# A two-block transformer kernel on one core: the MLP and the expert stage put in one program block, pooling means as band products on TensorE, tile 0's queries with tokens as the stationary operand

## The reference, cut to what matters

```python
m = square(relu(rms_norm(x, pre_mlp_g) @ mlp_w1)) @ mlp_w2      # first block's MLP
x = x + rms_norm(m, post_mlp_g)
h = concatenate([meta_tokens, x])                               # 16 + 256 rows

def pool_mixer(h, w_pool, scale):      # windows 2, 4, 8, 16, one for each 256 channels
    pooled = (c - c_prev) / minimum(pos + 1, w) - hg            # trailing mean minus self
    outs.append(einsum('bsc,cd->bsd', pooled, w_pool[g]))
    return concatenate(outs) * scale
h = h + pool_mixer(rmsnorm(h, norm_mix[0]), pool_w[0], pool_scale[0])

def peer(h, w_query, sub_keys, u, v):  # 8 heads, 2 x 128 sub-keys, 16 experts of 16384
    q = (h @ w_query) as (token, head, half, 128)
    s = einsum('bthpc,hpnc->bthpn', q, sub_keys)                # then top-16 of each half,
    ...                                                         # top-16 of their 256 sums
    return einsum('btk,btkd->btd', gate * gelu(u[expert] . h), v[expert])
h = h + peer(rmsnorm(h, norm_ffn[0]), peer_wq[0], peer_keys[0], peer_u[0], peer_v[0])
```

## Time and profile before

| | |
|---|---|
| median of 3 runs | 1946.3 us (1945.75 to 1946.77) |
| the profiled execution, its time | 1945.45 us |
| its span, first to last instruction | 1943.7 us |
| PE, DVE, ACT, POOL busy | 72%, 59%, 31%, 27% of the span |
| moved by DMA | 669.98 MB, mean 345 GB/s |
| chain that ended last | DMA 35%, PE 19%, DVE 13% |

### The profile page before, as it was taken

One profiled execution on the slowest core, in us unless ns is written; L12 is line 12 of the kernel. 1 busy time (PEld: TensorE's weight loads), 2 busy tenths in 40 slices (PEclk: granted clock), 3 DMA queues, 4 the chain that ended last, 5 costly groups with the idle time before them and its releaser, 6 DMA issues.

```text
span 1943.7 us, 20478 instructions
## 1 busy us (share of the span) xinstructions
PE 1406.8 (72%) x6422; PEld 591.3 (30%) x6422; DVE 1154.7 (59%) x2667; ACT 604.8 (31%) x1567; POOL 519.5 (27%) x572
## 2 busy tenths in 40 slices
PE   6978999968666655658967786578678865556565
PEld 5835666557223210112312232122132221101010
DVE  2551000073787766676678655776786568777764
ACT  2041111122334322334344332333444233232332
POOL 2000000001434333333233332323333233333332
PEclk9988999968888876669977897789778886776666
DMA  9022345314999999999999999999999999999997
GB/s 336 34 112 98 139 163 205 140 54 177 420 421 421 421 419 420 420 419 403 417 420 387 400 418 419 421 390 417 420 396 406 418 422 417 421 421 421 421 422 292
DMA packets 113366, 669.98 MB, mean 345 GB/s; under 512 B 11359, under 2 KB 12513, under 8 KB 44401
## 3 DMA queue, kind: packets, MB, share of 16 engines
q0 software_dynamic: 76032, 553.68, 69.0%
q1 hardware_dynamic: 37232, 115.09, 15.6%
HBM read 667.68 MB, written 1.05 MB: 344 GB/s over the span
## 4 chain that ended last, share of the span: by engine, by line
DMA 35%; PE 19%; DVE 13%; ACT 4%; issue 3%; DVEq 2%; POOL 2%; ACTq 1%; POOLq 0%
DMA big<-in_peer_uv,expert 32%; PE ps L558 7%; DVE big L571 6%; PE ps L719 6%; DMA normed<-in_peer_uv,expert 3%; DVEq L457 2%; PE ps L345 2%; POOL big L524 2%; PE ps L543 1%; ACT placed L603 1%; DMA big<-in_w_kv 1%; ACT placed L607 1%; ACT L579 1%; PE ps L723 1%; ACT L603 1%
## 5 line engine op out<-in xcount | busy, mean ns | idle before, releaser
L558 PE MATMUL ps<-big,placed 128*32 128x512 f32 (+1 forms) x2056 | 625.3, 809 | 417.2 <-ACT placed L607 415.1
L571 DVE CUSTOM_DVE_ANT_0 big<-big,ps 128x1024 f32<-128x1024 f32 x514 | 613.9, 1219 | 333.7 <-DMA big<-in_peer_uv,expert 317.2
L524 POOL DMA_INDIRECT big<-in_peer_uv,expert x514 | 489.7, 953 | 980.5 <-PE ps L558 874.0
L603 ACT ACTIVATE placed<-sel,dots 128x32 f32<-128x32 f32 (+1 forms) x528 | 168.3, 319 | 815.5 <-DVE dots L571 808.3
L558 PEld LDWEIGHTS ps<-big,placed 128*32 128x32 f32 (+1 forms) x2056 | 83.6, 122 | 861.0 <-ACT placed L607 780.2
L719 PE MATMUL ps<-big 128*128 128x512 f32 x384 | 189.3, 630 | 11.0 <-DVE big L1041 4.7
L607 ACT ACTIVATE placed<-placed,gate 128x32 f32<-128x32 f32 (+1 forms) x528 | 169.5, 321 | 37.1 <-issue 1.0
L230 DVE RECIPROCAL stats<-stats 128x1 f32<-128x1 f32 (+1 forms) x17 | 2.7, 162 | 253.3 <-ACT stats L224 252.8
L1538 PE MATMUL ps<-ua,big 128*128 128x256 f32 x512 | 116.7, 383 | 0.0
L1549 PE MATMUL ps<-big,sc 128*128 128x512 f32 x256 | 114.4, 592 | 0.0
L719 PEld LDWEIGHTS ps<-big 128*128 128x128 f32 x384 | 70.2, 197 | 126.3 <-issue 108.3
(11 more groups left out here) (296 smaller groups left out, 1242.2 us busy)
## 6 DMA issues: line engine op xcount, KB each, us to landing
big<-in_mlp_w SPq DMA_DIRECT2D x16, 2048.0 KB, 7.8
big<-in_w_kv SPq DMA_DIRECT2D x32, 512.0 KB, 15.5
big<-in_peer_wq SPq DMA_DIRECT2D x32, 512.0 KB, 13.5
big<-in_w_in SPq DMA_DIRECT2D x5, 2048.0 KB, 17.7
big<-in_peer_uv,expert POOLq DMA_INDIRECT x514, 15.3
big<-in_peer_wq SPq DMA_DIRECT2D x1, 8192.0 KB, 27.3
big<-in_w_q SPq DMA_DIRECT2D x16, 512.0 KB, 10.8
big<-in_w_o SPq DMA_DIRECT2D x16, 512.0 KB, 11.8
```

The source lines that it names most:

```text
L524: nc.gpsimd.indirect_dma_start(out=pair_row(n), out_offset=None, in_=rows, in_offset=bass.IndirectOffsetOnAxis(ap=expert[:, n // TOPK % DE ...
L558: last = nc.tensor.matmul(acc[r:r + tokens, :], placed[:, n % RING, 0:tokens], pair_row(n)[:, D + BANK * half:D + BANK * (half + 1)], star ...
L571: nc.vector.tensor_tensor_reduce(out=row, in0=row, in1=rows_x, scale=1.0, scalar=0.0, op0=ALU.mult, op1=ALU.add, accum_out=dots[:, u % 2, ...
L603: a.activation(to, same, ACT.Gelu, scale=dots[:, u % 2, k:k + 1])
```

## The change

- The MLP block and the expert block become one: no barrier, and work of the second can stand ahead of, or among, the end of the first. POOL builds four band matrices (and their parts for the 16 rows before a tile) while the MLP runs; the meta rows are normed then too, ACT's part of it ahead of its release of the `up` banks to PE. SP's loads of `pool_w`, the scale, the `ffn0` gain and the keys move ahead, each behind a wait for its buffer.
- Pooling: transposes, copies, doublings and ratio go. PE takes the normed rows as the stationary operand against the band matrix (128 columns) and, for the 16 rows before the tile, a second small one (16 columns), `pool_sums`; the result is the pooled and transposed tile, and DVE only multiplies by the gain (`pooled_out`).
- Queries of x0: the 128 tokens are the stationary operand and 512 columns of `peer_wq` move (`query_rows_pe`), 2 banks for each half of the heads; ACT brings them out, PE transposes them back by 128 x 128 (`query_columns_pe`), ACT and DVE bring those out. Unit 0's scores stand after the first half.
- The meta queries leave the head. They are products of 16 columns, four in each of the quarters 2 to 5; the meta scores stand in quarter 6, and x1's queries move from quarters 4 to 19 to quarters 6 to 21. x1's norm stands on DVE after unit 0's `route`, its transposes are PE's last work of the head, its copies stand in quarter 1.
- POOL waits ahead of slots 4, 6 and 7 for what these buffers held.

```diff
-        def act_squares(act, tiles, after, tag):
...
+        def act_squares(act, rows, t, tag, scratch):
+            step(act, nc.scalar.activation(scratch[0:rows], h[0:rows, t, :], ACT.Square,
+                                           accum_out=stats[0:rows, t:t + 1]), tag + "_squares")
+            act_root_mean(act, rows, t, tag)
...
+        def ffn0_transposes_out(dve, n):
...
+            dve.wait_ge(S("ffn0_t"), n + 1)
+            if t == NT:
+                nc.vector.tensor_copy(hnt[:, :, 0:META], cut(bank(b), 0, KD, META)).then_inc(S("ffn0_t_out"), 1)
+                return
+            for j in range(2):
+                nc.vector.tensor_copy(hnt[:, 4 * j:4 * j + 4, at:at + P], cut(bank(b + j), 0, 4, P))\
+                    .then_inc(S("ffn0_t_out"), 1)
...
+        def query_rows_pe(pe, half):
+            if half:
+                pe.wait_ge(S("ffn0_scores_out"), 1)
+            for b in range(2):
+                at = D * half + BANK * b
+                for k in range(KD):
+                    last = nc.tensor.matmul(bank(6 + b), hnt[:, k, META:META + P], wq_peer[:, k, at:at + BANK],
+                                            start=(k == 0), stop=(k == KD - 1))
+                last.then_inc(S("q_rows_done"), 1)
+        def query_rows_act(act, half):
+            for b in range(2):
+                act.wait_ge(S("q_rows_done"), 2 * half + b + 1)
+                nc.scalar.activation(query_rows[half][:, BANK * b:BANK * (b + 1)], bank(6 + b), ACT.Copy)\
...
+        def query_columns_pe(pe, half):
+            if half:
+                pe.wait_ge(S("q0_out"), 2)
+            for b in range(2):
+                pe.wait_ge(S("q_rows"), 2 * half + b + 1)
+                for c in range(4):
+                    hp = 4 * b + c
+                    last = nc.tensor.transpose(bank(4 + b)[:, P * c:P * (c + 1)],
+                                               query_rows[half][:, P * hp:P * (hp + 1)], ident[:])
+                last.then_inc(S("q0_t"), 1)
...
+        def late_query(t, hp):
+            return (hp, 0, META) if t == NT else (2 * PH + hp, META + P, P)
...
+            n, at, cols = late_query(t, hp)
             if n >= 2:
                 pe.wait_ge(S("ffn0_q_out"), n - 1)
             for k in range(KD):
-                last = nc.tensor.matmul(bank(4 + hp % 2)[:, 0:cols], wq_peer[:, k, P * hp:P * (hp + 1)],
+                last = nc.tensor.matmul(bank(4 + n % 2)[:, 0:cols], wq_peer[:, k, P * hp:P * (hp + 1)],
                                         hnt[:, k, at:at + cols], start=(k == 0), stop=(k == KD - 1))
             last.then_inc(S("ffn0_q_done"), 1)
...
+            n, at, cols = late_query(t, hp)
+            act.wait_ge(S("ffn0_q_done"), n + 1)
+            head = hp // 2
+            to = q_meta[:, hp % 2, head, META * head:META * (head + 1)] if t == NT else qt[:, hp, at:at + cols]
+            nc.scalar.activation(to, bank(4 + n % 2)[:, 0:cols], ACT.Copy).then_inc(S("ffn0_q_out"), 1)
...
+            if n < META_UNIT:
+                pe.wait_ge(S("q0_out"), 2 * half + 2)
+            else:
+                pe.wait_ge(S("ffn0_q_out"), q_ready)
...
-            pe_transposes(pe, LAYER0_TILES, "ffn0")
+            ffn0_transposes(pe, 0)
+            pe.wait_ge(S("ffn0_t_out"), 2)
+            pe.wait_ge(S("peer_wq0_loaded"), 16)
+            query_rows_pe(pe, 0)
+            ffn0_transposes(pe, 1)
+            query_columns_pe(pe, 0)
+            pe.wait_ge(S("keys0_loaded"), 16)
+            scores0_pe(pe, 0)
+            query_rows_pe(pe, 1)
+            query_columns_pe(pe, 1)
+            scores0_pe(pe, 1)
...
             unit_rows(pe, 0)
-            for n in range(2, 9):
-                scores0_pe(pe, n, 2 * PH)
+            for n in range(2, META_UNIT):
+                scores0_pe(pe, n)
+            ffn0_transposes(pe, 2)
...
+            for n in range(2):
+                act.wait_ge(S("h1"), n + 1)
+                act_squares(act, *FFN0_TILES[n][0:2], "ffn0", ua[:, 0:D])
+            query_rows_act(act, 0)
+            query_columns_act(act, 0, 0)
+            scores0_act(act, 0)
+            act.wait_ge(S("h1"), 3)
+            act_squares(act, *FFN0_TILES[2][0:2], "ffn0", sc[:, 1024:2048])
+            query_rows_act(act, 1)
+            for b in range(2):
+                query_columns_act(act, 1, b)
+            for n in range(1, META_UNIT):
                 scores0_act(act, n)
...
-        LATE_QUERIES = 4
+        LATE_META, LATE_QUERIES = 2, 6
...
+            if LATE_META <= x < LATE_META + 4:
+                if x == LATE_META:
+                    pe.wait_ge(S("ffn0_t_out"), 5)
+                    pe.wait_ge(S("q_meta_zeroed"), 1)
+                for i in range(4):
+                    queries0_pe(pe, NT, 4 * (x - LATE_META) + i)
             hp = x - LATE_QUERIES
+            if hp == 0:
+                scores0_pe(pe, META_UNIT, 2 * PH)
...
+                if n == 4:
+                    pool.wait_ge(S("q0_t"), 4)
                 if n == 6:
-                    pool.wait_ge(S("ffn0_scores_done"), META_UNIT + 1)
+                    pool.wait_ge(S("ffn0_normed"), 3)
+                if n == RING - 1:
+                    pool.wait_ge(S("ffn0_t"), 3)
...
+            ffn0_norm(dve, 2)
...
+                    if (s, j) == (0, 1):
+                        ffn0_transposes_out(dve, 2)
...
+                sp.wait_ge(S("up_done"), DFF // P - FT)
+                sp.dma_start(poolw, pool_w[0].rearrange("g (k p) n -> p (g k) n", p=P)).then_inc(S("pool_w_loaded"), 16)
+                sp.wait_ge(S("down_done"), DFF // P)
+                sp.dma_start(scale_row, pool_scale[0].partition_broadcast(P)).then_inc(S("scale_loaded"), 16)
+                sp.wait_ge(S("down_done"), DFF // P + FT)
+                sp.dma_start(ffn0_row, norm_ffn[0].partition_broadcast(P)).then_inc(S("ffn0_gain_loaded"), 16)
+                sp.wait_ge(S("x2"), NT)
+                sp.dma_start(gb[:, :, :].rearrange("p a n -> p (a n)"), peer_keys[0]).then_inc(S("keys0_loaded"), 16)
+                sp.wait_ge(S("ffn0_scores_done"), L0_UNITS)
...
+                for i in range(POOL_GROUPS):
+                    w = 2 ** (i + 1)
+                    for to, cols in ((band, P), (before, META), (meta_before, META), (meta_band, META)):
+                        band_step(g.memset(to[:, i, :], 1.0 / w))
+                    for to, cols, base in ((band, P, 0), (meta_band, META, 0)):
+                        band_step(g.affine_select(out=to[:, i, :], in_=to[:, i, :], compare_op=ALU.is_ge, fill=0.0, base=0,
+                                                  pattern=[[1, cols]], channel_multiplier=-1))
+                    for to, cols, apart in ((band, P, 0), (before, META, P), (meta_before, META, META), (meta_band, META, 0)):
+                        band_step(g.affine_select(out=to[:, i, :], in_=to[:, i, :], compare_op=ALU.is_ge, fill=0.0,
+                                                  base=w - 1 - apart, pattern=[[-1, cols]], channel_multiplier=1))
+                    band_step(g.affine_select(out=band[:, i, :], in_=band[:, i, :], compare_op=ALU.not_equal,
+                                              fill=1.0 / w - 1.0, base=0, pattern=[[-1, P]], channel_multiplier=1))
...
+                act.wait_ge(S("meta_loaded"), 16)
+                act_squares(act, META, NT, "pool", sc[:, 3072:3072 + D])
...
+                pool_norm(0, META, NT, hnm)
+                dve.wait_ge(S("gain1_loaded"), 16)
+                scaled(0)
+                added(0)
+                scaled(1)
+                pool_norm(1, P, 0, hn[:, 0, :])
+                added(1)
+                pooled_out(0, 1)
+                pool_norm(2, P, 1, hn[:, 1, :])
+                pooled_out(0, 2)
+                dve.wait_ge(S("scale_loaded"), 16)
+                add_mixed(0)
+                pooled_out(1, 3)
+                pooled_out(2, 4)
+                pooled_out(2, 5)
+                dve.wait_ge(S("ffn0_gain_loaded"), 16)
+                ffn0_norm(dve, 0)
+                ffn0_transposes_out(dve, 0)
+                add_mixed(1)
+                add_mixed(2)
+                ffn0_norm(dve, 1)
+                ffn0_transposes_out(dve, 1)
+                query_columns_dve(dve, 0, 1)
+                peer_vector(dve)
...
+                def pool_sums(n):
...
+                    for k in range(KD):
+                        cols = slice(P * k, P * (k + 1))
+                        if t == NT:
+                            last = m.matmul(bank(4)[:, META * k:META * (k + 1)], hnm[:, cols], meta_band[:, k // 2, :],
+                                            start=True, stop=True)
+                            continue
+                        to = bank(6 + k // 4)[:, P * (k % 4):P * (k % 4 + 1)]
+                        m.matmul(to, hn[:, t, cols], band[:, k // 2, :], start=True, stop=False)
+                        last = m.matmul(to[:, 0:META], earlier[:, cols], apart[:, k // 2, :], start=False, stop=True)
```

(14 more changed lines are left out.)

328 lines of the change are left out of this document (134 added, 194 removed).

## The result

The changed kernel takes **1960.9 us** (median of 4 runs, 1958.5 to 1961.6) against 1946.0 for the kernel before on the same chip (4 runs, 1945.4 to 1946.8): a ratio of 1.0074, 95% interval 1.0056 to 1.0091. It is slower by 15 us where 13 us less were forecast. The profiled execution took 1961.45 us, its span is 1959.7; that of before is 1943.7.

A forecast was written before the change was run, and what follows sets the result against it. It took the DMA fetch stream as the bound: its start and whether it runs dry. Gains 14.1 + 2.6 less 3 make 13.7, booked as 13.0, so median 1933.3 us; forecast range 1929.5 to 1938.

The forecast's parts named there:

- The rule it read first: Whole kernel: faster arithmetic in the loop buys nothing; what counts is when the fetch stream begins and whether it runs dry.
- The failed term: Loop quarters 2 to 5: meta queries moved there cost the stream 3 us, with ends of 0 and 24.
- At full clock the following quarters keep pace: Quarters after the first with meta queries: 9.5 us of PE each against the stream's 10.0; at half clock each loses 6.
- The price of an instruction: Meta queries in quarters 2 to 5: a 16-column instruction costs 0.08 us at full clock, 0.13 at half.
- the slot values: Quarters 2 to 5 on PE: four cost 4.2 us at full clock, 7.7 at half.
- rival (d): Quarters 2 to 5: clock stays at 0.50, 16 us a quarter, 24 us lost against 16.7 gained, 1953 us; chance 0.05.
- the start of the band products: Head, pooling: PE can start its first band product at about 392.3 us.
- the chain behind them: Head, after the first query rows: bank copy, transposes, copy, scores, copy, from 432.2 to 435.1 us for `route`.
- x0's sums: Head, pooling: x0's band products take 6.0 us at half clock, within 4.0 to 8.0.
- I take full clock from about 399: Head, pooling: PE working without a break from 392.3 reaches full clock then; x0's pool products take 3.5 us.
- The charge of 1.8 us: Head, query rows: added to each half for a lower clock after the break at the copies, 3.6 in all.
- The unit rows: End of the head, PE: rows of unit 0 take 1.9 us, as before, ahead of six units' scores.

The follow-up runs named there:

- the filled kernel: Changed kernel with the operands of x0's second band product filled with zero rows from 16 to 128 partitions, meta queries left in quarters 2 to 5: 1960.5 us, 1.0095.
- the 144-column experiment: Changed kernel with each meta query product of quarters 2 to 5 moving 144 columns instead of 16, only 16 kept: 1942.6 us, ratio 0.9980.
- riding, wide sums: Changed kernel with meta queries moved along with x1's, x0's second band operands zero-filled to 128 partitions, and that product moving 128 columns: 1927.6 us, ratio 0.9928.
- five kernels with unfilled sums and the new query rows: Changed kernel 1960.9 us; its variants without meta queries 1937.6, with 144-column meta queries 1942.6, meta queries behind slot values 1971.2, meta queries moved with x1's 1940.4.
- the old queries (unfilled and filled): Changed kernel's pooling with tile 0's queries as before the change: 1958.3 us; the same with x0's second band operands zero-filled to 128 partitions: 1949.3 us.
- the four filled kernels with the new query rows: Zero-filled x0 operands on the changed kernel 1960.5 us; with meta queries moved with x1's 1930.8; on that, 128 moving columns 1927.6, or x0's transposes first 1932.5.
- the kernel whose loop kept pace: Changed kernel with meta queries moved along with x1's and x0's second band operands zero-filled to 128 partitions: 1930.8 us, 0.9945, against 0.9968 without the filling.

## Why the prediction was wrong, step by step

**The rule it read first** holds: when the stream begins, and whether it runs dry. The table above puts a number on it, and every span follows it.

**The failed term: the meta queries, "3 us lost, with ends of 0 and 24".** Measured 22.5. The step that failed is the clock: "At full clock the following quarters keep pace" supposed that a busier PE gets it. The trace has PE busy 40.00 of 40 us at 0.59, and at 0.50 in the filled kernel. Where the clock was full in this place (144 columns), a quarter took 10.6 us and the stream lost 3.4.

The price of an instruction, 0.08 and 0.13 us, was wrong too. It was read from transposes of 16 partitions and 16 columns, the nearest row by its columns and the wrong one: band products show 0.214 at half and 0.113 at full clock, with 16 columns or with 128, when both operands have 128 partitions. That is 1.6 and 1.4 times the price taken. But the slot values were priced too high, by a row of a single one: four in a run take 2.6 us at full clock and 3.6 at half, not 4.2 and 7.7. The two errors nearly cancel, and that was luck: a quarter is 7.2 + 2.6 = 9.8 us at full clock (an estimate from these rows; no run has 16 columns at full clock there) where 9.5 was forecast, and 17.3 at half, measured in the filled kernel, where 16.0 was. The Trainium skill, "TensorE: Matmul & The Clock Gate", Part 2, LDWEIGHTS, which prices a weight load by the stationary operand's columns whatever moves, was set aside for that row. At full clock these rows side with it: 0.113 us measured against an estimate of 0.107 from its formula for 128 columns, and no change from 16 to 128 moving columns. At half clock they show twice its figure.

**That was rival (d)**: PE at half clock for most of quarters 2 to 5, 14.0 to 17.3 us a quarter for its 16, decision once more than 17 us are lost. It had a chance of 0.05, argued down with queries in a row that gave 1.00 after 4 us. But those had 144 columns; the 144-column experiment gets its 1.00 in this very place, the 16-column ones do not. Its time, 1953, was 8 us short because the head gained less than it assumed: 24 lost against 16.7 gained there, 22.5 against some 6 here.

**The head.** Right: the start of the band products (7.1 us behind the MLP for 7.0), the query rows (14.0 for 14.1), the chain behind them. Wrong: x0's sums 10.05 for 6.0, outside the stated 4.0 to 8.0, because the price was sought between zero and the 128-column one, and alternating with a 16-partition operand costs more than either; and "I take full clock from about 399", worth 2.7 in x0's pool products, 3.1 in x1's sums and 2.3 in the last ones. The charge of 1.8 us for each half of the query rows was not needed. Together the query rows begin 12.4 us late, and the pooling saves nothing up to there. The first fetch comes 3.6 us earlier than before, counted from the MLP's end, and not 14.1. The kernel with both repaired (riding, wide sums) has its query rows 31.9 us behind the MLP (31.0 forecast), its first fetch 60.3 (61.3), its first dot product 73.9 (76.5), and a ratio of 0.9928 where the forecast was 0.9935. So the working of the chain was sound, and two prices and the clock were not.

**The unit rows** took 3 us longer than before in the changed kernel, with "issue" ahead of four groups of L606 between 462 and 465; the forecast had them at 1.9. They take 5.2 to 5.4 us in all five kernels with unfilled sums and the new query rows, 9.0 and 9.5 with the old queries (unfilled and filled), and 1.93 in the four filled kernels with the new query rows. So the filling alone does not remove it. What does was not tried.

Not settled: the cause of these waits, and what keeps the clock up in pooling in one execution of the unfilled sums and not in others.

## What to carry to other kernels

Price a small matmul by both operands: what it moves may cost nothing, and what it loads may be all of it; a row for a price must have the same partitions on both sides, not the same column count. Before work of narrow products is moved into a loop that has slack "on PE", work its time out at half clock, and let it ride as extra columns on a product that is there anyway. And test an earlier start against the first refill of the ring: here the same filling, a first fetch 8 us earlier, was worth some 4.5 us in the kernel whose loop kept pace and nothing in the one whose loop did not.

## What the runs showed of the chip that was not expected

Moving 144 columns instead of 16 made a stretch with PE always busy faster by 18 us: the granted clock was 1.00 against 0.59. The same happened in pooling: with 128 columns in x0's second product the clock rose 5 us behind the first product, with 16 after 12. In the changed kernel it also fell again, from 1.00 to 0.50 at 409.2 us, without a pause of PE.

An instruction of 16 columns cost as much as one of 128, 0.214 us at half and 0.113 at full clock, with a stationary operand of 128 x 128. Filling an operand from 16 to 128 partitions with zeros made a pair of products cheaper, 0.85 us instead of 1.26.
